# Gated linear attention's first four chunks, placed two units later in the cycle of the feed-forward units

## The reference

```python
def gla_chunked(q, k, v, g, S0):
    def step(S, inp):
        qc, kc, vc, gc = inp
        Bc = jnp.cumsum(gc, axis=1)
        o_inter = jnp.einsum('blhd,bhdv->blhv', qc * jnp.exp(Bc), S)
        decay = jnp.exp(jnp.where(causal, Bc[:, :, None] - Bc[:, None, :], -jnp.inf))
        A = jnp.einsum('blhd,bshd,blshd->bhls', qc, kc, decay)
        o_intra = jnp.einsum('bhls,bshv->blhv', A, vc)
        BL = Bc[:, -1]
        S_new = jnp.exp(BL)[..., None] * S + jnp.einsum('bshd,bshv->bhdv', kc * jnp.exp(BL[:, None] - Bc), vc)
        return S_new, o_inter + o_intra
```

## Time and profile before

| | |
|---|---|
| median of 3 runs | 2677.02 us (2676.64 to 2677.27) |
| time of the profiled execution | 2676.7 us |
| its span | 2674.9 us |
| PE busy | 2620.0 us, 98% |
| DVE busy | 1495.6 us, 56% |
| ACT busy | 1006.0 us, 38% |
| mean granted TensorE clock | 0.993 of full speed |

### The profile page before, as it was taken

One profiled execution on the slowest core, in us unless ns is written; L12 is line 12 of the kernel. 1 busy time (PEld: TensorE's weight loads), 2 busy tenths in 40 slices (PEclk: granted clock), 3 DMA queues, 4 the chain that ended last, 5 costly groups with the idle time before them and its releaser, 6 DMA issues.

```text
span 2674.9 us, 38298 instructions
## 1 busy us (share of the span) xinstructions
PE 2620.0 (98%) x15999; PEld 2373.1 (89%) x15999; DVE 1495.6 (56%) x2301; ACT 1006.0 (38%) x1439; POOL 0.2 (0%) x4
## 2 busy tenths in 40 slices
PE   8999999999999999999999999999999999999996
PEld 6899898877988998899898988998886989999996
DVE  5644475655476763366654775327776386444435
ACT  4343355442343433344424344325352344222222
POOL 0000000000000000000000000000000000000000
PEclk9999999999999999999999999999999999999998
DMA  6454454444433323433223243343336333322222
GB/s 211 140 177 144 140 171 134 134 138 143 142 122 124 121 80 129 146 127 91 91 80 122 94 153 114 132 150 108 111 90 192 123 122 130 107 87 79 86 80 87
DMA packets 182168, 331.25 MB, mean 124 GB/s; under 512 B 19917, under 2 KB 99405, under 8 KB 181997
## 3 DMA queue, kind: packets, MB, share of 16 engines
q1 hardware_dynamic: 181996, 328.81, 38.3%
HBM read 272.48 MB, written 56.28 MB: 123 GB/s over the span
## 4 chain that ended last, share of the span: by engine, by line
PE 85%; DVE 8%; ACT 5%; issue 2%; DMA 1%; SPq 0%; ACTq 0%; DVEq 0%
PE ps L864 76%; PE ps L1037 2%; ACT w_hi L1145 1%; DVE w_lo L1456 1%; DVE Y L1516 1%; DVE Y L1549 1%; DVE n_xs L1552 1%; DVE evicted L1500 1%; PE ps L1118 1%; PE ps L990 1%; PE ps L978 1%; DMA w_stage<-w_in_in 1%; PE ps L972 1%; PE ps L1067 1%; PE ps L1064 1%
## 5 line engine op out<-in xcount | busy, mean ns | idle before, releaser
L864 PE MATMUL ps<-HH,w_lo 128*128 128x288 f32 (+1 forms) x3696 | 1024.1, 331 | 12.5 <-DVE HL L1952 7.4
L864 PE MATMUL ps<-HH,w_hi 128*128 128x288 f32 (+1 forms) x3696 | 1009.6, 328 | 0.0
L864 PE MATMUL ps<-HL,w_hi 128*128 128x288 f32 (+1 forms) x3696 | 1009.4, 328 | 0.0
L864 PEld LDWEIGHTS ps<-HH,w_lo 128*128 128x128 f32 x3696 | 630.8, 189 | 74.2 <-issue 13.8
L864 PEld LDWEIGHTS ps<-HL,w_hi 128*128 128x128 f32 x3696 | 629.9, 189 | 49.2
L864 PEld LDWEIGHTS ps<-HH,w_hi 128*128 128x128 f32 x3696 | 629.8, 189 | 47.2 <-issue 0.2
L1456 DVE TENSOR_TENSOR w_lo<-w_stage,w_hi 128x1024 fp32r<-128x1024 f32 x396 | 483.7, 1222 | 287.0 <-ACT w_hi L1145 285.9
L1145 ACT ACTIVATE w_hi<-w_stage 128x1024 fp32r<-128x1024 f32 x396 | 416.0, 1052 | 332.1 <-PE ps L864 314.1
L1516 DVE TENSOR_TENSOR Y<-ps,Y 128x512 f32<-128x512 f32 (+1 forms) x320 | 227.0, 721 | 152.7 <-PE ps L864 152.2
L864 PE MATMUL ps<-hid_hi,w_lo 128*128 128x288 f32 (+1 forms) x1056 | 293.8, 333 | 11.4 <-DVE Y L1516 10.6
L864 PE MATMUL ps<-hid_lo,w_hi 128*128 128x288 f32 (+1 forms) x1056 | 289.1, 328 | 0.0
(11 more groups left out here) (195 smaller groups left out, 1605.4 us busy)
## 6 DMA issues: line engine op xcount, KB each, us to landing
w_stage<-w_in_in SPq DMA_DIRECT2D x100, 512.0 KB, 3.7
w_stage<-w_gate_in SPq DMA_DIRECT2D x88, 512.0 KB, 3.5
w_stage<-w_up_in SPq DMA_DIRECT2D x88, 512.0 KB, 3.5
w_stage<-w_down_in SPq DMA_DIRECT2D x88, 512.0 KB, 3.5
w_stage<-w_out_in SPq DMA_DIRECT2D x32, 512.0 KB, 3.6
proj_scratch<-evicted SPq DMA_DIRECT2D x48, 288.0 KB, 2.2
proj_scratch<-evicted SPq DMA_DIRECT2D x48, 256.0 KB, 2.1
n_xs<-x_scratch SPq DMA_DIRECT2D x3, 2304.0 KB, 9.1
```

The lines of the kernel that those rows point to most:

```text
L864: mm = pe.matmul(ps[:, grp.bank + t, 0:W], wsl(w, k), x[:, k, t * W:(t + 1) * W], start=(k == first and m == 0), stop=(k == last and m == 2))
```

## The change

One list of slots is changed. Chunk c of GLA over block 0 (c = 0 to 3) stood on G(8+2c), the even gate unit of its cycle, and now stands on D(3+c,1), the second half of the down projection two units later. So in each cycle `le` and the next chunk's `la1` go from G odd to G even, `lvt` and `la2` from U odd to D(b,0), `la3` and `la` from G even to D(b,1), `l1` from D(b,0) to U even, `l2` from D(b,1) to G odd, and `lb` from U even to U odd. `la1` and `la2` of chunk 0 move from P(23) and P(24) to G(8) and D(3,0); `lload`, its loads, stays on P(22). The last `le` moves from G(15) to G(16). GLA over block 1 and everything else stay.

```diff
@@ -240,7 +240,7 @@
     assert u < at["P", 1, 0, 0, 0] - 1, (u, at["P", 1, 0, 0, 0])
     for h in range(H):
         tag(at["P", 1, 0, 5, 0] + 2 * h, "lg", 0, h)
-    u = gla(plan, 0, at["P", 1, 0, 22, 0], [at["G", 0, 1, i, 0] for i in (8, 10, 12, 14)])
+    u = gla(plan, 0, at["P", 1, 0, 22, 0], [at["D", 0, 1, b, 1] for b in (3, 4, 5, 6)])
     assert u <= at["W", 1, 0, 0, 0], (u, at["W", 1, 0, 0, 0])
     u = at["W", 1, 0, KD - 1, 0]
     tag(u - 6, "xload", 5)
```

## The result

| | before | after |
|---|---|---|
| median | 2676.83 us (4 runs, 2676.34 to 2677.27) | 2696.09 us (4 runs, 2690.01 to 2698.65) |
| ratio | | 1.0069, 95% interval 1.0056 to 1.0082 |
| profiled execution | 2676.7 us | 2696.57 us |

The account below looks back on a forecast made before the run. PE, busy 98% of the span, was taken as the bound, so only waits between its matmuls could change. New losses 16.2 + 2.9 + 1.6 + 8.8 + 4.2 = 33.7 us, less 16.6, gave +17.1: 2694.0 us, range 2681 to 2702.

Parts of the forecast that it names:

- What goes, 16.6 us in D(3,0) to D(6,0): First down halves: the waits there vanish once `la3` and `la` leave G even, a gain of 16.6 us.
- D(4,0) to D(6,0), 5.4 us each: `le` and `la1` before these units delay group 2 by 4.1 us and group 3 by 1.3, 16.2 us in all.
- D(3,0), 2.9 us by `hi` and `lo`: In D(3,0), ACT's work behind G(8) delays `hi`, `lo` and so group 3: 2.9 us lost.
- Second halves, 2.2 us each: Each D(b,1): `la2` on DVE between the halves makes group 2 late, 2.2 us four times, 8.8 us.
- D(7,0), 1.6 us: In D(7,0), only the last `le` stands before it and delays group 2: 1.6 us lost.
- The moved loads and PE steps at no cost: `la`, `l1`, `l2`, `lb` and SP's loads in their new units: priced at nothing.
- The clock, 4.2 us: D(4,0) to D(6,0): a clock fall in each new gap slows group 3 by 1.4 us, 4.2 us together.
- Rival of the slow clock, 2705: Half clock lasts into the second halves' groups 0 and 1; clock term 15 us, total +28, 2705; chance 0.12.
- Rival of the fast side: DVE reaches group 0 of D(b,0) in time, removing both waits there: -3.3 to -8 us, 2669; chance 0.05.

Follow-up runs that it names:

- Experiment 4: The kernel before, with GLA's first four chunks over block 0 one unit earlier and the first loads on P(21): 2659.20 us, ratio 0.9934.
- Experiments 3 and 8: The kernel after with chunk 0 back on G(8): 2689.73 us; the kernel after with `la1` of chunks 1 to 3 on D(b,0): 2694.01 us.
- experiment 2: The kernel after, with DVE making `lo` before the last output of every D unit instead of before the second: 2692.61 us, ratio 1.0056.
- experiment 1: The kernel after, with `la2` of block 0's chunks on the gate unit G even with `la1` instead of on D(b,0): 2694.03 us, ratio 1.0062.
- the second profiled execution: The kernel after, run again with no edit and profiled: 2696.09 us.
- Experiment 6: The kernel after, with chunks 0 to 3 one unit earlier, on D(3,0) to D(6,0): 2681.51 us, ratio 1.0022.

## Why the prediction was right

Forecast 2694.0, measured 2696.09: 17.1 us more were forecast, and 19.3 were measured. By its steps:

- **What goes, 16.6 us in D(3,0) to D(6,0).** Right. Experiment 4 takes these waits away with nothing in their place and gains 16.7 us.
- **D(4,0) to D(6,0), 5.4 us each.** Right, and the points in it too: group 2 at +7.26 (7.3 forecast), group 3 at +10.20 (10.2). U(9)'s steps in the trace of before were a true copy of what would come before D(4,0). Experiments 3 and 8 show that this takes `le` and `la1` together: group 2 starts at +3.2 with `la1` alone and at +4.6 with `le` alone.
- **D(3,0), 2.9 us by `hi` and `lo`.** Right by experiment 2, which takes it to nothing.
- **Second halves, 2.2 us each.** Group 2 at +5.28 (5.25 forecast). Right by experiment 1.
- **D(7,0), 1.6 us.** 8.0 us, forecast 8.0.
- **The moved loads and PE steps at no cost.** No wait for V, for a weight or at the level products shows in the stretch.
- **The clock, 4.2 us.** The mechanism was right and this term too small. The nine units lost 36.2 us, 29.5 of them at full clock by the sum, so the clock took some 6.7. I had put one slow group on each of D(4,0) to D(6,0). In the profile D(4,0) has its slow group 3 (3.26 us), while D(5,0) has half of one (2.44) and D(6,0) lost 0.2 only; but D(3,0), D(5,1) and D(6,1), which I had left at full clock, lost 1.4 each. Waits of 1.9 to 2.9 us can also bring it down, and not each time: behind the same 2.94 us D(3,0) kept full clock in the second profiled execution.
- **Rival of the slow clock, 2705.** Not so: the clock fell behind the gaps of some 4 us. It was back before the second half began in D(5,0) and D(6,0), and in group 0 of D(4,1) after the fall in D(4,0). The Trainium skill, TensorE: Matmul & The Clock Gate, section on oscillation, says that idle gaps which come back in every turn of a loop put the engine back to half rate each time. For the falls the trace agrees, with granted clocks of 0.82 to 0.88 in all first halves but D(7,0). They cost 6.7 us beside 29.5 us of waits, about a quarter.
- **Rival of the fast side.** It needed `la1` to end by +2.4, and it ended at +6.5 (1223.00 less 1216.54), to the tenth as in the rows.

## What to carry to other kernels

A step that is moved between engines' queues should be judged at the unit behind it: ask for each PSUM group who takes it, what that engine has queued before, and when. Here the same steps cost 16.6, 36.2, about 22 or 0 us by a shift of one or two units, and the free place is the one where PE has its own small products beside the other engines' work. Here a trace in which the steps already stood next to some other unit gave the new timings to a tenth of a microsecond. Experiment 6 missed its range by 16 us because one queue had not been asked: ACT's, with `la1`'s exponentials before `hi` and the gate's output.

## What the runs showed of the hardware

The granted clock fell to the half level behind waits as short as 1.9 us (D(5,1) and D(6,1) of the kernel after, 0.83), but not behind each of them (D(4,0) of the kernel before, 1.94 us and 1.00). Behind the 1.2 us of D(7,0) it stayed at 1.00; the 0.95 and 0.88 of D(3,1) and D(4,1) are slow matmuls at their start, from the fall in the half before. A fall shows as 3.26 instead of 1.85 us for 12 matmuls of 288 columns, 1.4 us; where a later group is waiting anyway, as group 2's slowness in D(6,0), it costs nothing. The level products of 64 columns took 4.16 instead of 3.52 us when some of them ran at it. A fall can therefore turn a wait that was removed into a slow group that was hidden before, as experiment 2 shows in D(4,0) to D(6,0).
